# Moving two pairs of ones-products for the residual gates in a two-layer decoder trunk

## The reference, cut to what matters

```
mod = silu(c) @ ada_w[i] + ada_b[i]          # 6 parts of 1024
sh1, sc1, g1, sh2, sc2, g2 = split(mod, 6)
h = rms_norm(x, norm_mix_g[i]) * (1 + sc1) + sh1
x = x + g1 * mixer(h)
h = rms_norm(x, norm_mlp_g[i]) * (1 + sc2) + sh2
x = x + g2 * sq_relu_mlp(h, w1[i], w2[i])
```

## Time and profile before

| | us |
|---|---|
| median of 3 runs | 657.33 (657.2 to 658.45) |
| profiled execution | 658.41 |
| its span, first to last instruction | 656.6 |
| VectorE (DVE) busy | 473.6 |
| ScalarE (ACT) busy | 340.2 |

### The profile page before, as it was taken

One profiled execution on the slowest core, in us unless ns is written; L12 is line 12 of the kernel. 1 busy time (PEld: TensorE's weight loads), 2 busy tenths in 40 slices (PEclk: granted clock), 3 DMA queues, 4 the chain that ended last, 5 costly groups with the idle time before them and its releaser, 6 DMA issues.

```text
span 656.6 us, 9233 instructions
## 1 busy us (share of the span) xinstructions
PE 618.6 (94%) x3471; PEld 516.3 (79%) x3471; DVE 473.6 (72%) x658; ACT 340.2 (52%) x581; POOL 39.9 (6%) x66
## 2 busy tenths in 40 slices
PE   4689999898899999999997999999799999999997
PEld 2457865676889988998965777788598999899985
DVE  4448998887778978979876987865787654555465
ACT  3256632647744355534438777564875443554440
POOL 3120011000000101101000000000000000000000
PEclk9799999999999999999999999999999999999999
DMA  8999799664588998999964645344357555555501
GB/s 289 352 391 396 255 318 338 221 242 161 182 312 316 377 364 310 378 356 330 340 256 160 209 145 192 130 129 129 128 183 272 187 192 192 192 192 192 192 0 64
DMA packets 58941, 156.97 MB, mean 239 GB/s; under 512 B 2802, under 2 KB 3296, under 8 KB 58912
## 3 DMA queue, kind: packets, MB, share of 16 engines
q1 hardware_dynamic: 47008, 112.41, 48.4%
q0 software_dynamic: 11904, 44.19, 19.2%
HBM read 155.54 MB, written 1.05 MB: 238 GB/s over the span
## 4 chain that ended last, share of the span: by engine, by line
PE 71%; DVE 10%; ACT 7%; DMA 6%; issue 3%; SPq 2%; ACTq 0%; DVEq 0%
PE ps L481 14%; PE ps L482 13%; PE ps L483 13%; PE ps L642 8%; PE ps L641 8%; PE ps L640 8%; DMA w_raw<-in_gla_w_in_dram 6%; DVE w_lo L1343 2%; ACT arena L1049 2%; ACT w_hi L986 2%; SPq L389 1%; DVE ada_acc L1361 1%; ACT arena L1008 1%; PE ps L562 1%; DVE arena L1420 1%
## 5 line engine op out<-in xcount | busy, mean ns | idle before, releaser
L986 ACT ACTIVATE w_hi<-w_raw 128x1024 fp32r<-128x1024 f32 x192 | 201.6, 1057 | 231.4 <-PE ps L483 118.3
L1343 DVE TENSOR_TENSOR w_lo<-w_raw,w_hi 128x1024 fp32r<-128x1024 f32 x192 | 232.6, 1222 | 123.2 <-ACT w_hi L986 123.1
L481 PE MATMUL ps<-w_hi,a_hi 128*128 128x512 f32 x288 | 119.6, 415 | 16.6 <-DVE a_lo L1491 14.6
L640 PE MATMUL ps<-a_hi,w_hi 128*128 128x256 f32 x448 | 127.0, 284 | 0.0
L642 PE MATMUL ps<-a_hi,w_lo 128*128 128x256 f32 x448 | 126.9, 283 | 0.0
L641 PE MATMUL ps<-a_lo,w_hi 128*128 128x256 f32 x448 | 126.9, 283 | 0.0
L482 PE MATMUL ps<-w_lo,a_hi 128*128 128x512 f32 x288 | 113.5, 394 | 0.0
L483 PE MATMUL ps<-w_hi,a_lo 128*128 128x512 f32 x288 | 113.5, 394 | 0.0
L481 PE MATMUL ps<-w_hi,m_hi 128*128 128x512 f32 x256 | 100.2, 392 | 0.0
L482 PE MATMUL ps<-w_lo,m_hi 128*128 128x512 f32 x256 | 99.9, 390 | 0.0
L483 PE MATMUL ps<-w_hi,m_lo 128*128 128x512 f32 x256 | 99.7, 390 | 0.0
(11 more groups left out here) (186 smaller groups left out, 506.2 us busy)
## 6 DMA issues: line engine op xcount, KB each, us to landing
w_raw<-in_mlp_w_dram SPq DMA_DIRECT2D x64, 1024.0 KB, 5.7
ada_raw<-in_ada_w_dram POOLq DMA_DIRECT2D x40, 1024.0 KB, 6.2
w_raw<-in_gla_w_in_dram SPq DMA_DIRECT2D x12, 1024.0 KB, 16.7
w_raw<-in_moba_w_in_dram SPq DMA_DIRECT2D x12, 1024.0 KB, 6.7
ada_raw<-in_ada_w_dram SPq DMA_DIRECT2D x4, 1024.0 KB, 14.3
arena<-in_ada_w_dram SPq DMA_DIRECT2D x4, 1024.0 KB, 15.7
w_raw<-in_gla_w_out_dram SPq DMA_DIRECT2D x4, 1024.0 KB, 7.4
w_raw<-in_moba_w_out_dram SPq DMA_DIRECT2D x4, 1024.0 KB, 4.9
```

The lines of the kernel that those rows point to most:

```text
L481: mm(out, hi, w_hi[:, slot, wc], start=first, stop=False)
L640: mm(o, w_hi[:, u, w], a_hi[:, a, :], start=u == 0 and k == 0, stop=False)
L986: A(w_hi[:, c % SPLIT], w_raw[:, c // 2, c % 2], ACT.Copy).then_inc(hi_made, 1)
L1343: V.tensor_tensor(w_lo[:, c % SPLIT], w_raw[:, c // 2, c % 2], w_hi[:, c % SPLIT].bitcast(F32), ALU.subtract).then_inc(lo_made, 1)
```

## The change

In layer 0 TensorE computes the pair behind the second unit of the out-projection's first half, and VectorE adds the biases after the last two `a_lo`. In layer 1 TensorE computes the pair between the two tiles of block 0, ahead of `turn_norm(2, 1)`, once the second tile's residual has left banks 6 and 7, and into these banks; VectorE adds the biases at the start of `moba`, before the four `w_lo` of block 1; and the wait for `gate_ok` 6 moves from `turn_rot(0)` to the start of block 1, which writes banks 6 and 7.

```
@@ TensorE, layer 0
                 turn_o(0)
+            def mix_gates():
                 pe.wait_ge(on_ok, 2)
                 for i in range(2):
                     fin_gate(4 + i, 2 + i)
@@ TensorE, layer 1
-                def gate1():
-                    pe.wait_ge(a_ok, A_NORM[2] + 8)
+                def gates_and_turn():
+                    pe.wait_ge(x_new, x_done(2, 1, 1))
                     for i in range(2):
-                        fin_gate(16 + i, 2 + i)
+                        fin_gate(16 + i, 6 + i)
+                    turn_norm(2, 1)
                 def turn_rot(n):
                     pe.wait_ge(rot_ok, n + 1)
-                    if n == 0:
-                        pe.wait_ge(gate_ok, 6)
                 def after(n, u):
-                    if (n, u) == (1, 0):
-                        gate1()
@@ ahead of each block
+                    if n == 1:
+                        pe.wait_ge(gate_ok, 6)
-                        project_tiles(u0, banks, A_NORM[2], {(0, 3): lambda: turn_norm(2, 1)})
+                        project_tiles(u0, banks, A_NORM[2], {(0, 3): gates_and_turn})
@@ the out-projection of layer 0
-                    out_project({0: lambda: turn_o(1), 3: lambda: sum_mods(1, 4)},
+                    out_project({0: lambda: turn_o(1), 1: mix_gates, 3: lambda: sum_mods(1, 4)},
@@ VectorE, layer 0
                 gated(1)
+                o_low(0, range(2, 4))
                 for i in range(2):
                     gate(i, 2 + i)
-                o_low(0, range(2, 4))
                 for _ in range(2):
                     ada()
@@ VectorE, layer 1
-                def gate1():
-                    for i in range(2):
-                        gate(4 + i, 2 + i)
                     if (n, u) == (0, 3):
                         tables()
-                        gate1()
+                for i in range(2):
+                    gate(4 + i, 6 + i)
                 for n in range(1, 8):
```

## The result

The changed kernel takes 662.72 us (median of 8 runs, 660.83 to 666.66) against 658.42 (8 runs, 657.20 to 660.21): ratio 1.0060, 95% interval 1.0042 to 1.0078, so it is slower by 2.8 to 5.1 us. Its profiled execution took 661.81, span 660.0.

A forecast was written before the change was run, and what follows sets the result against it. TensorE was taken to bound the kernel, busy 618.6 of 656.6 us. Layer 0's 2.5 plus layer 1's 1.0 gave 3.5, added to the median 657.33: 660.8 us; range 659.0 to 663.0, with 0.3 for the spread of runs.

The forecast's parts named there:

- The price of a pair: Two moved products take 1.71 us of TensorE's dense stream; VectorE's two additions take 1.29.
- the first pair's removal: Start of layer 0's out-projection: removal only lengthens TensorE's wait for `a_lo` from 1.77 to 3.5 us; gain 0.
- The first pair's insertion: Layer 0, behind unit 2: late additions delay `ada()`, `sum_mods` and the second half's first `w_lo`; 2.5 us late.
- The second pair: Layer 1, before the second tile's transposes: these start 1.4 us late; after later waits 1.0 stays.
- The sum: Whole kernel: 2.5 + 1.0 = 3.5 us slower, 660.8 on the median; chance 0.55.
- the stated range: Whole time, from 659.0 (VectorE free) to the clock's 663.0, and 0.3 for the spread of runs.
- the clock: Rival: TensorE's clock halves after the 3.5 us wait at layer 0's out-projection, costing 2.2 more; 663.0; chance 0.20.
- The forecast's own range: Whole time, 660.0 to 661.8 us, from the bounds of the two parts taken one at a time.
- VectorE's delays cost nothing: Rival: `ada()` and turnings have more slack; layer 0 costs 1.7, layer 1 draws or gains 0.3; 659.0; chance 0.15.
- The norm takes all in: Rival: norm chains keep their own time and absorb the delays, block 1 loses 1.71; 655.6; chance 0.05.
- a draw: Rival: layer 0 costs 1.7 and layer 1 gives 1.7, its second tile's norm coming later; 657.3; chance 0.05.

The follow-up runs named there:

- e3: Layer 0's half of the change alone, with VectorE's two additions moved behind the last two `ada()`; layer 1 as before; 661.51 us, ratio 1.0041 to the kernel before.
- e2: Kernel before with only layer 1's half of the change, layer 0 untouched; 658.97 us, ratio 1.0003.
- e9: Kernel before with layer 1's pair behind the second tile's transposes, and computed again, unused, ahead of the first turning; 658.31 us, ratio 0.9998.
- e12: Kernel before with layer 1's pair just ahead of the first turning, additions behind block 2's last `w_lo`; 657.70 us, ratio 0.9988.
- after: The changed kernel itself, both layers' edits, against the kernel before; 662.72 us, ratio 1.0060.
- e1: Kernel before with only layer 0's half of the change, layer 1 untouched; 662.98 us, ratio 1.0061.
- e11: The changed kernel run again, on the same chip as its form with both waits filled; 663.16 us, ratio 1.0088 to the kernel before.
- e7: Kernel before plus three unused products in TensorE's wait before layer 0's first block; 657.83 us, ratio 1.0007.
- e8: Kernel before plus six unused products, in the wait before layer 0's first block and the waits ahead of it; 659.88 us, ratio 1.0028.
- e6: Kernel before with layer 1's pair behind the second tile's transposes, additions behind that tile's first two `a_lo`; 659.77 us, ratio 1.0022.
- e10: The changed kernel with unused pairs filling the waits at the out-projection's start and before the first turning; 662.22 us, ratio 1.0061 to the kernel before.

## Why the prediction was right, and where it was not

**The price of a pair and the first pair's removal.** Right. In the stream the pair takes 1.72 (358.17 to 359.89; forecast 1.71), and the wait at the out-projection grew by just that, to 3.49 where 3.5 was forecast. VectorE's idle time before `a_lo` grew by the time of the two additions that had stood there, from 1.26 to 2.45.

**The first pair's insertion, 2.5.** Right in each step: `ada()` forecast at 138.8, measured at 138.75; first `w_lo` 144.0 and 143.98; `sum_mods` 144.15 and 144.11; first product of the second half 145.3 and 145.34. A is 2.64 longer. e3 splits it as the working did.

**The second pair, 1.0.** Right: transposes 1.41 late (1.4), the first turning 1.35 (1.4), the second 0.93 (0.97), the third 1.35 (1.4), the probabilities 0.93 (0.97), and B +0.85. The alternation between the chain through TensorE and that through ScalarE's reading is in the waits of 1.78, 0.26, 0.81 and 1.22. e2 gives the same 0.85 alone. What was expected of a pair in a real wait, 0.3 to 0.5 gained in B, also held, in e9 and e12.

**The sum.** 3.5 was forecast, and A and B give 2.64 + 0.85 = 3.49. The profiled executions differ by 3.40.

**The time, and luck in it.** The median, 662.72, is 1.9 above the 660.8 forecast. 1.1 of it is the base: the kernel before has 658.42 over 8 runs, not the 657.33 of the first 3. The other 0.8 is the difference of the medians, 4.3, against 3.5 in the traces; what makes it is open. The time is inside the stated range only because that range reached up to the clock's 663.0. The forecast's own range does not hold it, and it was added up wrongly: the bounds of the two parts, one at a time, give 657.33 + 2.2 = 659.5 to 657.33 + 4.7 = 662.0, not 660.0 to 661.8.

**The clock.** This was the rival, held apart with 0.20. It is not another case but an addition to the first, present in some traces and not in others. Of four traces with the unfilled wait at 130 us (after, e1, e3, e11) two show the fall; of the ten in which products fill it none does. If filling did nothing, both falls would lie in those four by chance about once in 15 times (6 of 91 pairs), so the link to the wait is likely and not proven, the more so as e7 and e8 show falls elsewhere. That the medians differ by 4.3 rather than 3.5 has room for falls, but their share is not proven. The price of one had been put at 2.2, and was 2.82 in e1 and 2.49 in e3 (32.51 less 30.90 - 0.88). The 2.2 took 4.4 us of products at half the clock, seen at the head only up to 30 us; in e1 they last from 129.89 to 136.0, and half of these 6.1 us, 3.05, is near what was lost. The place it was taken from could not show a price: in that trace the low clock was off the chain. The argument against the rival, that nowhere else so low a clock is recorded, falls with e7 and e8. I also missed that the change opens a second place: the wait before the first turning grew to 1.78, and in e6, at 2.15, the clock fell behind it, for 1.57.

**The other rivals.** "VectorE's delays cost nothing" falls with e3 and with the 0.59 before L523. "The norm takes all in" and "a draw" fall with B.

## What to carry to other kernels

A wait that is to hide work must be measured at its own place: 0.31 could not hide 1.71, while the wait of 0.37 in front of the first turning could (e12), because moving the work out of the stream ahead of it made that wait longer by the same amount. When a product moves, look at the engine that consumes it: its next work is queued behind the new wait, and that was 0.88 of the 2.64 of layer 0 here. And work that fills a wait of 2 to 3.5 us may be what holds TensorE's clock. A fall of 1.6 to 2.8 us is as large as the effect that is looked for, and it can stand anywhere in the program: compare stretches of the trace that hold the change, look at the granted clock in them and outside them, and take several runs.

## What the runs showed of the hardware

TensorE's granted clock fell from 2.4 to 1.2 GHz (0.50) in waits of 3.5 that followed eight transposes (e1, e3), after a wait of 2.15 followed by eight transposes (e6), after eight transposes and a wait of 1.43 (e7, e8), and after a wait of 1.69 and the products of L775 behind it (e7). The first two waits showed no fall where a pair of ones-products (four records) stood in them: ten traces at 130 us, three (e9, e10, e12) at 380. Transposes did not hold the clock in e1, e3, e6, e7 and e8. The Trainium skill, "TensorE: Matmul & The Clock Gate", "Part 4: PE-mode transpose", says that transposes do not count as busy in the same way; these five traces fit it, and no run here tests transposes alone. After equal code the clock fell in some executions and not in others: after and e11 against e1 at 130 us, twelve traces against two at 170. What one fall costs depends on its length and on what bounds the stretch: about 1.6 us for the short ones (3.4 us; e6, e7, e8), 2.5 to 2.8 for those of 6.8 us (e1, e3), nothing for 6.8 us at the head of the kernel before, which waits for loads there.
